# Weights in two rings, transfers of two row chunks, and a second queue: an inference step of a two-layer hybrid decoder

## The reference, cut to what matters

```python
def swiglu(x, wg, wu, wd):
    h = jax.nn.silu(jnp.einsum('bld,df->blf', x, wg)) * jnp.einsum('bld,df->blf', x, wu)
    return jnp.einsum('blf,fd->bld', h, wd)

def moe(x, w_router, wg, wu, wd):
    ...
    for e in range(N_EXPERTS):
        y = y + gates[..., e:e + 1] * swiglu(x, wg[e], wu[e], wd[e]).astype(jnp.float32)
```

## Time and profile before

| | |
|---|---|
| median of 3 runs | 1034.43 us (1032.98 to 1040.81) |
| the profiled execution | 1032.9 us, of which the span is 1031.1 us |
| TensorE busy | 942.6 us (91%) |
| VectorE, ScalarE, GpSimd busy | 720.1, 521.0, 142.2 us |
| mean granted clock of TensorE | 0.959 |
| moved by DMA | 224.86 MB, mean 218 GB/s |

### The profile page before, as it was taken

One profiled execution on the slowest core, in us unless ns is written; L12 is line 12 of the kernel. 1 busy time (PEld: TensorE's weight loads), 2 busy tenths in 40 slices (PEclk: granted clock), 3 DMA queues, 4 the chain that ended last, 5 costly groups with the idle time before them and its releaser, 6 DMA issues.

```text
span 1031.1 us, 14724 instructions
## 1 busy us (share of the span) xinstructions
PE 942.6 (91%) x6081; PEld 813.9 (79%) x6081; DVE 720.1 (70%) x821; ACT 521.0 (51%) x538; POOL 142.2 (14%) x176
## 2 busy tenths in 40 slices
PE   4999999999999989999889898998989799898974
PEld 4999899999999989988767586676757577575774
DVE  3785576555655778746677776976878777887853
ACT  5421454443444443224566656755666655766442
POOL 4226121101100453432000000000000000000013
PEclk9999999999999999989899899998999999999987
DMA  9944155586458476322488869896789959898801
GB/s 325 308 133 130 37 169 164 141 250 202 119 164 270 135 190 214 111 77 90 138 303 294 303 221 336 285 355 234 253 314 305 338 192 312 308 323 330 304 3 43
DMA packets 120823, 224.86 MB, mean 218 GB/s; under 512 B 5906, under 2 KB 90002, under 8 KB 120608
## 3 DMA queue, kind: packets, MB, share of 16 engines
q1 hardware_dynamic: 118688, 216.63, 62.6%
q0 software_dynamic: 2064, 7.23, 2.7%
HBM read 220.31 MB, written 3.99 MB: 218 GB/s over the span
## 4 chain that ended last, share of the span: by engine, by line
PE 54%; DMA 16%; DVE 15%; ACT 8%; issue 5%; POOL 2%; SPq 0%; DVEq 0%; ACTq 0%; POOLq 0%
PE bank L607 12%; PE bank L608 12%; PE bank L609 12%; DVE wlo L1250 9%; DMA raw<-in_moe_w_down 6%; ACT whi L1025 5%; DMA raw<-in_moe_w_up 5%; DMA raw<-in_moe_w_gate 4%; PE bank L880 2%; PE bank L881 2%; PE bank L882 2%; PE bank L798 1%; PE bank L799 1%; DVE hid L1540 1%; ACT hid L1107 1%
## 5 line engine op out<-in xcount | busy, mean ns | idle before, releaser
L1250 DVE TENSOR_TENSOR wlo<-raw,whi 128x1408 fp32r<-128x1408 f32 (+2 forms) x254 | 478.5, 1892 | 156.0 <-ACT whi L1025 154.3
L1025 ACT ACTIVATE whi<-raw 128x1408 fp32r<-128x1408 f32 (+2 forms) x254 | 395.6, 1567 | 203.5 <-PE bank L609 56.1
L607 PE MATMUL bank<-xh,whi 128*128 128x264 f32 x672 | 195.6, 291 | 14.7 <-DVE xl L1262 14.7
L608 PE MATMUL bank<-xl,whi 128*128 128x264 f32 x672 | 192.5, 286 | 0.0
L609 PE MATMUL bank<-xh,wlo 128*128 128x264 f32 x672 | 192.1, 286 | 0.0
L854 PE MATMUL bank<-whi,xeh 128*96 128x512 f32 (+1 forms) x384 | 145.1, 378 | 5.9 <-ACT hid L1107 2.9
L856 PE MATMUL bank<-whi,xel 128*96 128x512 f32 (+1 forms) x384 | 144.6, 377 | 0.0
L855 PE MATMUL bank<-wlo,xeh 128*96 128x512 f32 (+1 forms) x384 | 144.1, 375 | 0.0
L607 PEld LDWEIGHTS bank<-xh,whi 128*128 128x128 f32 x672 | 128.7, 191 | 16.7 <-DVE wlo L1250 10.9
L608 PEld LDWEIGHTS bank<-xl,whi 128*128 128x128 f32 x672 | 128.8, 192 | 0.3
L609 PEld LDWEIGHTS bank<-xh,wlo 128*128 128x128 f32 x672 | 128.1, 191 | 0.0
(11 more groups left out here) (225 smaller groups left out, 1380.4 us busy)
## 6 DMA issues: line engine op xcount, KB each, us to landing
raw<-in_moe_w_gate SPq DMA_DIRECT2D x64, 704.0 KB, 5.8
raw<-in_moe_w_up SPq DMA_DIRECT2D x64, 704.0 KB, 5.5
raw<-in_moe_w_down SPq DMA_DIRECT2D x40, 1024.0 KB, 7.6
raw<-in_w_in SPq DMA_DIRECT2D x20, 1024.0 KB, 9.6
raw<-in_ffn_w_down SPq DMA_DIRECT2D x16, 704.0 KB, 4.6
raw<-in_ffn_w_gate SPq DMA_DIRECT2D x10, 1024.0 KB, 5.7
raw<-in_ffn_w_up SPq DMA_DIRECT2D x10, 1024.0 KB, 5.4
raw<-in_w_o SPq DMA_DIRECT2D x8, 1024.0 KB, 5.6
```

Of the source, the lines that this page charges most:

```text
L607: pe.matmul(out, w_hi, x_hi, start=start, stop=False)
L608: pe.matmul(out, w_hi, x_lo, start=False, stop=False)
L1025: act.activation(whi[u % SPL][:, 0:n], raw[u % RAW][:, 0:n], ACT.Copy).then_inc(hi_ready, 1)
L1250: dve.tensor_tensor(wlo[u % SPL][:, 0:n], raw[u % RAW][:, 0:n], whi[u % SPL][:, 0:n].bitcast(F32), ALU.subtract).then_inc(lo_ready, 1)
```

## The change

The slots become two rings. Raw columns and low halves share one of 17,408 columns, the low half being written over the raw columns it comes from; high halves have one of 7,168. Together that is the 24,576 columns of the twelve slots before. A function `ring` gives each load, and each unit in the high ring, the next free columns, and the unit whose use has to be over before they may be written. A transfer of raw columns now waits for TensorE's use of that unit (`unit_used`), where it waited for VectorE's low half before.

A transfer of gate, up or down rows brings two row chunks, and the units become single chunks: gate and up go in the order gate 0, gate 1, up 0, up 1, gate 2 and so on, and a down stage has 11 units of 1024 columns. The tables of what comes after which down unit are put in these units, at the same places. The transfers of up are begun by ScalarE (`load_up`, at the start of its step of the unit named in `UP_LOADS`); gate, down and all else stay with SyncE. A table `SPLIT_AT` says at which step a unit is split: as soon as the high ring has room, and at most 5,632 columns ahead of TensorE.

The tables that these functions give: the low ring holds eight dense units of 2048 or six pairs of 1408; in the expert stage most pairs may be loaded eight to ten units ahead of their use. The high ring holds three units of 2048, five of 1408 or seven of 1024, and the split runs four units of 1408 ahead.

```diff
-RAW = 4
-SPL = 4
+LOW_COLS, HIGH_COLS = 17408, 7168
+LANDINGS = 16
+LOOK = 5632
...
-DOWN = ((0, 2), (2, 2), (4, 2), (6, 2), (8, 2), (10, 1))
+DOWN = EC
...
+def ring(sizes, room):
+    at, taken, out = 0, [], []
+    for n in sizes:
+        if at + n > room:
+            at = 0
+        last = max((i for i, (a, b) in enumerate(taken) if a < at + n and at < b), default=-1)
+        out.append((at, last))
+        taken.append((at, at + n))
+        at += n
+    return out
+
+LOW_RING = ring([sum(COLS[u:u + n]) for u, n in LOADS], LOW_COLS)
+HIGH_AT, HIGH_LAST = zip(*ring(COLS, HIGH_COLS))
+for _i, (_u, _n) in enumerate(LOADS):
+    _at, _last = LOW_RING[_i]
+    LOAD_AFTER.append(max(sum(LOADS[_last]) if _last >= 0 else 0, *LOAD_AFTER[-1:], 0))
...
+def split_table():
+    out, first = {}, U_FF[1]
+    for v in range(first + AHEAD, U_PLE[1] + AHEAD):
+        u = max(HIGH_LAST[v] + 1, first)
+        while sum(COLS[u:v]) > LOOK:
+            u += 1
+        out.setdefault(min(u, U_PLE[1] - 1), []).append(v)
+    return out
...
-GATHER_AFTER = {0: 0, 2: 1, 3: 2, 4: 3}
-HID_AFTER = {1: (2, 0), 3: (1,)}
+GATHER_AFTER = {1: 0, 5: 1, 7: 2, 9: 3}
+HID_AFTER = {3: (2, 0), 7: (1,)}
...
-        raw = [place(f"raw{i}", [P, UNIT]) for i in range(RAW)]
-        whi = [place(f"whi{i}", [P, UNIT], F32R) for i in range(SPL)]
-        wlo = [place(f"wlo{i}", [P, UNIT], F32R) for i in range(SPL)]
+        raw = place("raw", [P, LOW_COLS])
+        wlo = place("wlo", [P, LOW_COLS], F32R, low_at)
+        whi = place("whi", [P, HIGH_COLS], F32R)
...
-                if vector_through is not None:
-                    sp.wait_ge(lo_ready, vector_through)
+                if LOAD_AFTER[i]:
+                    sp.wait_ge(unit_used, LOAD_AFTER[i])
...
-                        for k in range(DC):
-                            for i, src in enumerate((gate, up)):
-                                v = u + 2 * k + i
-                                load(v % RAW, v - (RAW - 1), src[k * P:(k + 1) * P, :], 1, FE)
+                        for k in range(0, DC, 2):
+                            load(u + 2 * k, gate[k * P:(k + 2) * P, :], 2, FE)
...
-                k, up = divmod(i, 2)
+                k, up = i // 4 * 2 + i % 2, i // 2 % 2
...
+            def load_up(u):
+                for e, k in UP_LOADS.get(u, ()):
+                    at = U_FF[1] + MOE_AT["gu", e] + 2 * k + 2
+                    i = LANDING[at]
+                    act.wait_ge(unit_used, LOAD_AFTER[i])
...
+                    act.dma_start(dst, src.rearrange("(k p) w -> p k w", p=P)).then_inc(raw_landed[i % LANDINGS], 16)
...
-                act.wait_ge(raw_landed[u % RAW], 16 * (u // RAW + 1))
-                if u >= SPL:
-                    act.wait_ge(unit_used, u - (SPL - 1))
+                i = LANDING[u]
+                act.wait_ge(raw_landed[i % LANDINGS], 16 * (i // LANDINGS + 1))
+                if HIGH_LAST[u] >= 0:
+                    act.wait_ge(unit_used, HIGH_LAST[u] + 1)
...
-                act.wait_ge(unit_used, U_FF[1] + MOE_AT["gu", e] + GU_UNITS - 1)
+                act.wait_ge(unit_used, U_FF[1] + MOE_AT["gu", e] + GU_UNITS - 2)
...
-                        split_next(MOE_AT[kind, e] + i + SPL - 1)
+                        load_up(U_FF[1] + MOE_AT[kind, e] + i)
+                        split_next(U_FF[1] + MOE_AT[kind, e] + i)
```

More of the change, by code:

```diff
@@ L196 @@
     MOE_AT[_kind, _e] = len(MOE_COLS)
-    MOE_COLS += [FE] * GU_UNITS if _kind == "gu" else [n * D for _, n in DOWN]
+    MOE_COLS += [FE] * GU_UNITS if _kind == "gu" else [D] * DOWN
 FF_UNITS = (STEP_UNITS, len(MOE_COLS))
@@ L215, with add_load, up_loads @@
 N_UNITS = U_MIX[DEPTH]
+PART_COLS = [(DC if kind != "down" else EC) * w * P for kind, _, w, _, _ in PART]
+COLS, LOADS = [], []
+def add_load(*cols):
+    LOADS.append((len(COLS), len(cols)))
+    COLS.extend(cols)
+for _l in range(DEPTH):
+    for _spec in W_IN + W_O:
+        add_load(_spec[2] * _spec[4])
+    if _l == 0:
+        for _w in PART_COLS * 2:
+            add_load(_w)
+    else:
+        for _kind, _e in PHASES:
+            if _kind == "gu":
+                for _ in range(DC):
+                    add_load(FE, FE)
+            else:
+                for _f in range(0, EC, 2):
+                    add_load(*[D] * min(2, EC - _f))
+    for _spec in PLEU:
+        add_load(_spec[2] * _spec[4])
+assert len(COLS) == N_UNITS
+def ring(sizes, room):
[10 more added lines that the diff above has]
+HIGH_AT, HIGH_LAST = zip(*ring(COLS, HIGH_COLS))
+LOW_AT, LANDING, LOAD_AFTER = [], [], []
+for _i, (_u, _n) in enumerate(LOADS):
+    _at, _last = LOW_RING[_i]
+    LOAD_AFTER.append(max(sum(LOADS[_last]) if _last >= 0 else 0, *LOAD_AFTER[-1:], 0))
+    for _j in range(_n):
+        LOW_AT.append(_at)
+        LANDING.append(_i)
+        _at += COLS[_u + _j]
+    assert _i < LANDINGS or LOAD_AFTER[_i] >= sum(LOADS[_i - LANDINGS])
+def split_table():
[6 more added lines that the diff above has]
+    return out
+SPLIT_AT = split_table()
+def up_loads():
+    out = {}
+    for e in range(NE):
+        for k in range(0, DC, 2):
+            u = U_FF[1] + MOE_AT["gu", e] + 2 * k + 2
+            out.setdefault(max(LOAD_AFTER[LANDING[u]], U_WO[1]), []).append((e, k))
+    return out
+UP_LOADS = up_loads()
 def chunk_table():
@@ L427, in program @@
         bank = [ctx.enter_context(nc.psum_tensor(f"bank{i}", [P, 512], F32)) for i in range(8)]
-        raw_landed = [sem(f"raw_landed{i}") for i in range(RAW)]
+        raw_landed = [sem(f"raw_landed{i}") for i in range(LANDINGS)]
         hi_ready, lo_ready, unit_used = sem("hi_ready"), sem("lo_ready"), sem("unit_used")
@@ L495, in h_final, with unit_raw, unit_lo, unit_hi @@
                 eng.wait_ge(acc_free, first + m + 1)
[L498 to L506, removed]
+        def unit_raw(u):
+            return raw[:, LOW_AT[u]:LOW_AT[u] + COLS[u]]
+        def unit_lo(u):
+            return wlo[:, LOW_AT[u]:LOW_AT[u] + COLS[u]]
+        def unit_hi(u):
+            return whi[:, HIGH_AT[u]:HIGH_AT[u] + COLS[u]]
         def y_bank(e):
@@ L537, in dense @@
                     m = t[name][layer]
-                    load(u % RAW, u - RAW + 1 if u >= RAW else None, m[k0 * P:(k0 + n) * P, c0:c0 + w], n, w)
+                    load(u, m[k0 * P:(k0 + n) * P, c0:c0 + w], n, w)
             def feed_forward():
@@ L547, in feed_forward @@
                         src = {"gate": gate, "up": up, "down": down}[kind]
-                        load((n.unit + i) % RAW, n.unit + (i - RAW + 1), src[:, c * P:(c + w) * P],
-                             EC if kind == "down" else DC, w * P)
+                        load(n.unit + i, src[:, c * P:(c + w) * P], EC if kind == "down" else DC, w * P)
             def experts():
@@ L553, in experts @@
                     u = U_FF[1] + MOE_AT[kind, e]
-                    gate, up, down = (t[name][0][e] for name in ("moe_w_gate", "moe_w_up", "moe_w_down"))
+                    gate, down = (t[name][0][e] for name in ("moe_w_gate", "moe_w_down"))
                     if kind == "gu":
-                        for k in range(DC):
-                            for i, src in enumerate((gate, up)):
-                                v = u + 2 * k + i
-                                load(v % RAW, v - (RAW - 1), src[k * P:(k + 1) * P, :], 1, FE)
-                    else:
-                        for i, (f, n) in enumerate(DOWN):
-                            load((u + i) % RAW, u + i - (RAW - 1), down[f * P:(f + n) * P, :], n, D)
+                        for k in range(0, DC, 2):
+                            load(u + 2 * k, gate[k * P:(k + 2) * P, :], 2, FE)
+                    else:
+                        for f in range(0, EC, 2):
+                            n = min(2, EC - f)
+                            load(u + f, down[f * P:(f + n) * P, :], n, D)
             dense(0, U_MIX[0], W_IN[:1])
@@ L871, in down @@
                     pe.wait_ge(hid_ready, 3 * NE)
[L872 to L882, removed]
+                if i % 4 == 0:
+                    pe.wait_ge(hl_ready, hid_turn(e, i // 4) + 1)
+                X, Y = hh[:, hid_slot(e, i), :], hl[:, hid_slot(e, i), :]
+                for half in range(2):
+                    b = bank[y_bank(e) + half][0:CAP, :]
+                    own = slice(half * 512, (half + 1) * 512)
+                    pe.matmul(b, X, H[:, own], start=(i == 0), stop=False)
+                    pe.matmul(b, X, L[:, own], start=False, stop=False)
+                    mm = pe.matmul(b, Y, H[:, own], start=False, stop=(i == EC - 1))
                 mm.then_inc(unit_used, 1)
@@ L892, in experts @@
                 for kind, e in PHASES:
-                    for i in range(GU_UNITS if kind == "gu" else len(DOWN)):
+                    for i in range(GU_UNITS if kind == "gu" else DOWN):
                         if kind == "gu":
@@ L1071, in feed_forward @@
                     for i, (kind, c, w, a, _) in enumerate(PART):
```

(13 more changed lines are left out.)

66 lines of the change are left out of this document (34 added, 32 removed).

## The result

The changed kernel takes 986.49 us in the median (985.82 to 987.42, 4 runs) against 1034.46 us: a ratio of 0.9526, with a 95% interval from 0.9485 to 0.9566. The forecast was 990 us. The profiled span is 985.2 us where it was 1031.1.

The account below looks back on a forecast made before the run. TensorE was taken as the bound, with late weight transfers idling it and lowering its clock in the expert stage. Waits 35.9 + clock 13 - smaller units 5 = 43.9 us off 1032.9, forecast 990 us, range 970 to 1018.

Parts of the forecast that it names:

- The lead: Expert stage: a pair's transfer begins eight to ten units ahead, 15 to 19 us, taking 35.9 us of waits away.
- The down waits: Expert stage, first down matmul waiting for low halves of its weights: all 19.8 us go, bounds 0 and 19.8.
- the gathers: Expert stage, gathers waiting for hidden rows, 10.7 us: 9.2 us go, 0.5 us left for each of three.
- The transposes: Expert stage, transposes waiting for the hidden steps, 4.0 us: half goes, bounds 0 and 4.0.
- Gate and up: Waits ahead of gate and up matmuls where expert 1 begins, 5.9 us: 4.9 us go, bounds 0 and 5.9.
- The clock: Expert stage, TensorE's mean clock of 0.96 costs 17.6 us: 13 us come back, a quarter stays.
- The 5 us charged for smaller down units: Down stages: short stalls on a tight VectorE, some 0.6 us for each of eight, bounds 0 and 20.
- ScalarE's queue: Gate and up stages: moving up transfers to ScalarE costs 0, bounds 0 and 4.2 us for each of seven, 29 us.
- the rival "better": Expert stage: all 58 us of idle time and lost clock go, 976 us or a little under; chance 0.08.
- The high ring: Dense units: three units of 2048 instead of four cost 0, bounds 0 and 4.2 us for each of 20 mixer units.
- The rival that named this part: Mixers: each of 20 units waits 4.2 us for room for high halves, 84 us in all, 1074 us; chance 0.06.
- The DMA rival: Expert stage: transfers become the bound at 314 GB/s, only 24 us off, 1010 us; chance 0.20.

Follow-up runs that it names:

- experiment 4: Low ring of the changed kernel cut from 17,408 columns to 11,264 (four pairs of 1408) or 14,080 (five pairs): 1018.06 us and 990.24 us.
- experiment 2: Changed kernel with the transfers of up put back on SyncE's queue in order of use, rings and two-row transfers kept: 983.20 us.
- experiment 6: Changed kernel with down units of two row chunks (2048 columns), six per expert instead of eleven: 989.32 us.
- experiment 5: Changed kernel splitting at most 4,224 columns ahead, three units of 1408, instead of 5,632: 980.03 us.
- experiment 7: Changed kernel with high ring restarted before layer 0's embedding and up on SyncE: 973.52 us; also splitting 4,224 ahead: 970.66; that with up on ScalarE: 970.11.

## Why the prediction was right, and where it wasn't

The time came within 4 us, but that is in part luck, the difference of two errors: the expert stage gave 56.4 us where 43.9 was forecast, and the embedding of layer 0 took 10.9 back (366.27 to 377.60 us, less the 0.4 us by which the first matmul of all was later) where nothing was.

- The lead, which carried the sum, was right, and experiment 4 shows it by taking it away. Of the four groups of waits, 40.4 us, 3.9 are left; 4.5 were forecast. The down waits went wholly, the gathers kept 1.0 of 1.5 us. The transposes kept none of the 2.0 left to them. Gate and up kept 2.9 us instead of 1.0: the late landing of experiment 2.
- The clock was mis-sized: 13 us were to come back, a quarter was to stay. The mean is 1.00 from 520 to 900 us, where it was 0.96, so nearly all of the 17.6 came. In the pair of experts shown, with one gap of 0.3 us, it is 1.00. The matmuls of the whole stage take 18.1 us less busy time.
- The 5 us charged for smaller down units were not paid. VectorE is busy 93 of 104 us in a pair of experts, as tight as forecast (88%), but TensorE waits for it only 0.3 us at a gather; and experiment 6 gains nothing from larger units.
- ScalarE's queue was taken at 0 with bounds of 0 and 29 us: it cost 3.3, by a mechanism the prediction had named (two transfers begun together land together), but had put on the gate pair and on every stage.
- The 58 us that could go "at most" were counted from 520 to 960 us alone. Over the whole stage TensorE was idle 42.9 us, and experiment 5 takes 63.2 us off it (486.9 to 423.7), so more could go than the rival "better" has (976 us): the best kernels here take 970 us, the lower end of the range.
- The high ring is the step that failed. It was taken at 0 on the ground that the ring holds three units of 2048 and that two units of TensorE's time stand over each split. At the embedding it held two. The rival that named this part put the price on the mixers, where the waits are unchanged. The place of each unit could have been worked out before any run from the `ring` function, which gave the lead too.
- The DMA rival fell: 336 GB/s over 380 us, and one wait of TensorE behind a landing. The 330 GB/s that the sum needed were there.

## What to carry to other kernels

Count how far ahead a transfer may begin in units of the consumer's time, and hold it against landing and preparation together: here a lead of 11 us cost 32 us of the run against one of 19 us, and a lead of 15 us only 4. In a ring with pieces of several sizes, look at every piece for how many places lie between it and the one it overwrites, not at room divided by size; the wrap can take one away just where sizes change. And work prepared further ahead than needed stands in front of urgent work in the same engine's list: here the fourth unit of lookahead cost 6.5 us, and 2.9 where the late landing was gone (experiment 7).

## What was unexpected in the hardware

Two transfers of 1.44 MB begun 10 ns apart on SyncE's and ScalarE's queues landed after 11.4 and 11.5 us, against medians of 7.1 and 7.6; one behind the other on SyncE's queue, the first landed after 8.0 us and the second after 11.1. So with the second queue one pair came 3.5 us later and the other no more than 0.2 us sooner (547.6 against 547.8 us). Transfers of 704 and of 1408 KB gave the same time (983.30 and 983.20 us) with several under way, the DMA moving 319 and 321 GB/s over the stage.
